# One program for routing and experts, and the last tile's work in another order: a mixture-of-experts layer on one core

## What is computed

```python
x = x + gt1 * (mixed @ w_out)                     # residual, kept in memory as x1
h = rmsnorm(x, g_ffn_norm) * (1 + sc2) + sh2      # kept in memory as h2
logits = h @ w_router + b_router
top_logits, top_idx = lax.top_k(logits, 4); wts = softmax(top_logits)
# for each expert e, for the tokens that chose it:
gu = h[tokens] @ w_gate_up[e] + b_gate_up[e]
act = min(glu, 7) * sigmoid(1.702 * min(glu, 7)) * (clip(lin, -7, 7) + 1)
x[tokens] += gt2 * wts * (act @ w_down[e] + b_down[e])
return rmsnorm(x, g_final)
```

## Time and profile before

| what | value |
|---|---|
| median of 3 runs | 2393.32 us (2392.87 to 2393.83) |
| the profiled execution's own time | 2393.82 us |
| its span, first to last instruction | 2392.2 us |
| PE busy | 2272.3 us (95%) |
| PEld, DVE, ACT, POOL busy | 65%, 40%, 14%, 36% |
| moved by DMA | 526 MB, mean 220 GB/s |

### The profile page before, as it was taken

One profiled execution on the slowest core, in us unless ns is written; L12 is line 12 of the kernel. 1 busy time (PEld: TensorE's weight loads), 2 busy tenths in 40 slices (PEclk: granted clock), 3 DMA queues, 4 the chain that ended last, 5 costly groups with the idle time before them and its releaser, 6 DMA issues. The chain is left out here.

```text
span 2392.2 us, 84238 instructions
## 1 busy us (share of the span) xinstructions
PE 2272.3 (95%) x33744; PEld 1559.7 (65%) x33744; DVE 957.4 (40%) x3183; ACT 335.9 (14%) x917; POOL 857.8 (36%) x1672
## 2 busy tenths in 40 slices
PE   6999999999999699999999999999999999999994
PEld 3878876555544367767777777776776667776563
DVE  2222226776356433333333333333333333333333
ACT  0000006776411100000000000000000000000001
POOL 1100004544214543434343434344443434444333
PEclk8999999999999799999999999999999999999997
DMA  9423042000234687476769494968869988989994
GB/s 314 163 90 109 1 121 71 2 1 2 77 119 145 222 313 278 143 270 210 272 212 340 147 341 145 342 207 297 313 229 384 349 285 303 380 292 390 391 370 160
DMA packets 195573, 526.26 MB, mean 220 GB/s; under 512 B 45416, under 2 KB 75264, under 8 KB 195328
## 3 DMA queue, kind: packets, MB, share of 16 engines
q1 hardware_dynamic: 142496, 479.22, 53.4%
q0 software_dynamic: 33808, 40.21, 8.2%
q10 hardware_dynamic: 19088, 4.47, 0.9%
HBM read 489.98 MB, written 33.35 MB: 219 GB/s over the span
## 5 line engine op out<-in xcount | busy, mean ns | idle before, releaser
L1670 PE MATMUL psum<-w_ring,xT 128*32 128x256 f32 x18304 | 1038.5, 380 | 28.5 <-issue 25.6
L1670 PEld LDWEIGHTS psum<-w_ring,xT 128*32 128x32 f32 x18304 | 693.7, 110 | 322.0 <-issue 48.6
L1682 PE MATMUL psum<-w_ring,actT 128*32 128x256 f32 x9152 | 528.7, 380 | 9.3 <-DMA w_ring<-in_w_down 7.7
L1682 PEld LDWEIGHTS psum<-w_ring,actT 128*32 128x32 f32 x9152 | 329.5, 110 | 166.0 <-DVE actT L1735 36.5
L1599 POOL TENSOR_TENSOR scalars<-scalars 128x1 f32<-128x1 f32 x578 | 109.9, 190 | 749.5 <-DVE xT L1739 657.4
L1717 ACT ACTIVATE sig<-glu 128x128 f32<-128x128 f32 x286 | 88.6, 310 | 1471.4 <-DVE glu L1726 1471.4
L1618 POOL DMA_INDIRECT x_rows<-y_out,scalars_i x145 | 233.9, 1613 | 43.7 <-issue 43.4
L1724 DVE TENSOR_TENSOR psum<-psum,up_bias 128x256 f32<-128x256 f32 x143 | 61.8, 432 | 410.3 <-PE psum L1670 400.1
L1748 DVE SCALAR_TENSOR_TENSOR y_out<-psum,scalars,gate_q 128x256 f32<-128x256 f32 x143 | 69.2, 484 | 300.0 <-PE psum L1682 220.9
L719 POOL TENSOR_SCALAR scores<-scores,coef 128x64 f32<-128x64 f32 (+5 forms) x128 | 133.5, 1058 | 147.7 <-DVE coef L926 147.7
L1608 POOL DMA_INDIRECT x_gathered<-h_rows,scalars_i x144 | 153.5, 1066 | 79.4 <-issue 77.4
(11 more groups left out here) (241 smaller groups left out, 2009.6 us busy)
## 6 DMA issues: line engine op xcount, KB each, us to landing
w_ring<-in_w_gate_up SPq DMA_DIRECT2D x256, 1024.0 KB, 16.0
w_ring<-in_w_down SPq DMA_DIRECT2D x128, 1024.0 KB, 19.9
ada_then_cmp_in<-in_w_ada SPq DMA_DIRECT2D x16, 1024.0 KB, 7.0
ada<-in_w_ada SPq DMA_DIRECT2D x8, 1024.0 KB, 6.9
xt<-in_x SPq DMA_DIRECT2D x8, 512.0 KB, 9.8
w_uv_then_w_out<-in_w_in SPq DMA_DIRECT2D x4, 1024.0 KB, 11.7
x_rows_in<-in_x SPq DMA_DIRECT2D x8, 512.0 KB, 4.2
x_rows<-x SPq DMA_DIRECT2D x8, 512.0 KB, 2.9
```

Of the source, the lines that this page charges most:

```text
L1670: last = nc.tensor.matmul(psU[h][j * BLK:(j + 1) * BLK, :], xT[:, k, :], w[:, j], start=(h == 0 and k == 0), stop=(k == KD - 1))
L1682: last = nc.tensor.matmul(psO[m * BLK:(m + 1) * BLK, :], actT[h][:, k, :], w[:, m * Q:(m + 1) * Q], start=False, stop=(h == 1 and k == KD ...
```

## The change

`experts` is no longer a block of its own. Its five streams become functions (`expert_loads`, `expert_rows`, `expert_products`, `expert_sigmoids`, `expert_gates`) that the streams of `route` call at their end, after a wait until `counts` is written (`s_order` at 3). The `AHEAD` counters and the three additions of nothing are gone, with what cleared and indexed them. DVE makes tile 7's residual before it transposes block 0. TensorE transposes tile 7's rows before the biases and half of block 0's second half. The first weighing waits for no addition.

```diff
@@ sync
+            sp.wait_ge(s_sc[i], 16 * TOPK * TILES // 2)
+        sp.wait_ge(s_order, 3)
+        sp.wait_ge(parts.s_xg, 16 * (FIRST + 1))
+        expert_loads(sp, parts)
@@ gpsimd
-                parts.gather(pool, 0)
-                pool.wait_ge(s_spare, 48)
-                parts.add_nothing(pool)
+                parts.gather(pool, 0, 1)
             if t == KNOWN_TILES + 3:
-                parts.add_rows(pool, 0, 4)
-                parts.gather(pool, 1)
+                parts.gather(pool, 1, 4)
         tiles(pool, body)
         scatter(TILES - 2, 0)
-        parts.add_rows(pool, 1, 10)
         scatter(TILES - 1, 1)
...
         parts.load_rows(pool, 0)
+        pool.wait_ge(s_spare, 48)
+        for i in range(2):
+            pool.wait_ge(s_x1st[i], 16 * TILES // 2)
         parts.take_rows(pool, 0)
         pool.wait_ge(parts.s_ids, 4)
-        parts.gather(pool, 2)
+        parts.gather(pool, 2, 7)
         parts.load_rows(pool, 1)
-        parts.add_rows(pool, 2, 16)
+        parts.add_rows(pool, 0, 10)
+        pool.wait_ge(s_order, 3)
+        expert_rows(pool, parts)
@@ tensor
         parts.up(pe, 0, 0)
+        transpose_h2(TILES - 1, 1)
         pe.wait_ge(s_bias, 6)
         pe.wait_ge(s_chain, base(TILES - 1) + 1)
         parts.up_bias(pe, 0)
         parts.up(pe, 0, 1, 0, KD // 2)
-        transpose_h2(TILES - 1, 1)
...
         parts.bias_and_down(pe, 0, 1)
+        pe.wait_ge(s_order, 3)
+        expert_products(pe, parts)
@@ scalar
+        act.wait_ge(s_order, 3)
+        expert_sigmoids(act, parts)
@@ vector
             residual(t, par)
+            if t == TILES - 1:
+                parts.transpose_x(dve, 0)
...
-            if t == KNOWN_TILES + 2:
-                parts.transpose_x(dve, 0)
...
-        ch.link(nc.vector.tensor_copy(counts[:], blocks_f[:]))
+        nc.vector.tensor_copy(counts[:], blocks_f[:]).then_inc(s_order, 1)
...
         parts.weigh(dve, 1)
-
+        dve.wait_ge(s_order, 3)
+        expert_gates(dve, parts)
@@ weigh
-        dve.wait_ge(s_y, b + AHEAD)
+        if not (isinstance(b, int) and b == 0):
+            dve.wait_ge(s_y, b)
...
-        dve.wait_ge(s_ysc, 16 * b + 16 * AHEAD + 16)
+        if not (isinstance(b, int) and b == 0):
+            dve.wait_ge(s_ysc, 16 * b)
@@ expert_rows (was the gpsimd stream of experts)
-                parts.gather(pool, first + i + 1)
-                parts.add_rows(pool, first + i + 1, 6 * (first + i) + 10)
+            parts.gather(pool, first + i + 1, 6 * (first + i) + 1)
+            parts.add_rows(pool, first + i - 1, 6 * (first + i) + 4)
```

More of the change, by code:

```diff
@@ L35 @@
 FIRST = 2
-AHEAD = 2
 KNOWN_TILES = 4
@@ L150, in layer_kernel @@
             stage3.close()
-            s_w = experts(nc, s4, parts)
         with ExitStack() as s5:
-            combine(nc, s5, sem, s_w, g_final, x1_d, out)
+            combine(nc, s5, sem, parts.s_w, g_final, x1_d, out)
 ADA_CHUNKS = 4
@@ L1494, in expert_parts @@
     HALF = D // 8
-    COLS = MAX_BLOCKS + EDGES + AHEAD + 1
+    COLS = MAX_BLOCKS + EDGES + 1
     xg = sb("x_gathered", [P, Q])
@@ L1507, in expert_parts @@
     ids_x, ids_y, zero_i = (cells_i[:, i:i + 1] for i in range(3))
-    quarter = sb("quarter", [P, 1 + AHEAD])
+    quarter = sb("quarter", [P, 1])
     rows_f = two("slot_rows", [P, EDGES, 2])
@@ L1599, in carry_waits, with gather @@
         nc.gpsimd.tensor_tensor(tick[:], zero[:], zero[:], ALU.add).then_inc(s_steps, 1)
-    def gather(pool, b):
-        done = 6 * b + 1
+    def gather(pool, b, done):
         pool.wait_ge(s_xT, b + 1)
         carry_waits(pool, done)
-        nc.gpsimd.tensor_tensor(ids_x[:], ids[:, bass.ds(b + AHEAD, 1)], zero_i[:], ALU.add).then_inc(s_steps, 1)
+        nc.gpsimd.tensor_tensor(ids_x[:], ids[:, bass.ds(b, 1)], zero_i[:], ALU.add).then_inc(s_steps, 1)
         carry_waits(pool, done + 2)
@@ L1646, in take_rows @@
         pool.wait_ge(s_quarter, e + 2)
-        nc.gpsimd.tensor_copy(ids[:, bass.ds(first + AHEAD, most)], rows_f[e % 2][:, bass.ds(skip, most), 0]).then_inc(s_ids, 1)
+        nc.gpsimd.tensor_copy(ids[:, bass.ds(first, most)], rows_f[e % 2][:, bass.ds(skip, most), 0]).then_inc(s_ids, 1)
         nc.gpsimd.tensor_copy(weight[:, bass.ds(first, most)], rows_f[e % 2][:, bass.ds(skip, most), 1]).then_inc(s_ids, 1)
@@ L1687, in bias_and_down @@
     def bias_and_down(pe, e, n):
-        pe.wait_ge(s_y, n + AHEAD)
+        if not (isinstance(n, int) and n == 0):
+            pe.wait_ge(s_y, n)
         for m in range(4):
@@ L1753, in expert_parts @@
         first_of, many_of, total, weights_of, load_weights, load_rows, load_first_rows, clear)
-    parts.gather, parts.add_rows, parts.add_nothing, parts.take_first_rows, parts.take_rows, parts.load_next, parts.up, parts.bias_and_down = (
-        gather, add_rows, add_nothing, take_first_rows, take_rows, load_next, up, bias_and_down)
+    parts.gather, parts.add_rows, parts.take_first_rows, parts.take_rows, parts.load_next, parts.up, parts.bias_and_down = (
+        gather, add_rows, take_first_rows, take_rows, load_next, up, bias_and_down)
     parts.load_bias, parts.load_gate, parts.sigmoids, parts.gates, parts.transpose_x, parts.weigh, parts.quarter, parts.s_c = (
@@ new lines, in expert_loads, with expert_rows @@
+def expert_loads(sp, parts):
+    for e in range(1, E):
+        w_up, w_dn = parts.weights_of(sp, e)
+        for c in range(CHUNKS):
+            sp.wait_ge(parts.s_w[c], 16 * e)
+            if e >= 2:
+                through = parts.first_of(sp, ENDS[e - 2] + 1)
+                sp.wait_ge(parts.s_spent[c], through)
+            parts.load_weights(sp, e, c, w_up, w_dn)
+def expert_rows(pool, parts):
+    first = parts.first_of(pool, 0)
+    for g in range(N_SEGMENTS):
+        many = parts.many_of(pool, g)
+        after = None
+        if g + 1 < N_SEGMENTS:
+            after = parts.take_rows(pool, g + 1)
+            parts.load_next(pool, g + 1)
+        with pool.Fori(0, many) as i:
+            parts.gather(pool, first + i + 1, 6 * (first + i) + 1)
+            parts.add_rows(pool, first + i - 1, 6 * (first + i) + 4)
+        first = after
+    last = parts.total(pool)
+    parts.add_rows(pool, last - 1, 6 * last + 1)
+    pool.wait_ge(parts.s_ysc, 16 * last)
+    pool.wait_ge(parts.s_xg, 16 * last + 16)
@@ new lines, in expert_products, with expert_sigmoids @@
+def expert_products(pe, parts):
+    for g, (e, part) in enumerate(SEGMENTS):
+        b = parts.first_of(pe, g)
+        many = parts.many_of(pe, g)
+        with pe.Fori(0, many) as i:
+            n = b + i
+            pe.wait_ge(parts.s_xT, n + 2)
+            parts.up(pe, e, 0)
+            parts.up_bias(pe, e)
+            parts.up(pe, e, 1)
+            parts.bias_and_down(pe, e, n)
+def expert_sigmoids(act, parts):
+    parts.load_bias(act, 1)
+    for g in range(N_SEGMENTS):
+        b = parts.first_of(act, g)
+        many = parts.many_of(act, g)
+        with act.Fori(0, many) as i:
+            parts.sigmoids(act, b + i)
+        if g in ENDS and ENDS.index(g) + 2 < E:
+            parts.load_bias(act, ENDS.index(g) + 2)
@@ new lines, in expert_gates @@
+def expert_gates(dve, parts):
+    for g in range(N_SEGMENTS):
+        b = parts.first_of(dve, g)
+        many = parts.many_of(dve, g)
+        dve.wait_ge(parts.s_ids, 2 * g + 4)
+        e = SEGMENTS[g][0]
+        at = HALF_OF[e]
+        dve.wait_ge(parts.s_bias[at], 64 * sum(HALF_OF[p] == at for p in range(e + 1)))
+        with dve.Fori(0, many) as i:
+            n = b + i
+            parts.gates(dve, n, 0, at)
+            parts.gates(dve, n, 1, at)
+            parts.transpose_x(dve, n + 1)
+            parts.weigh(dve, n)
```

88 lines of the change are left out of this document (6 added, 82 removed).

## The result

The changed kernel takes 2383.62 us (median of 7 runs, 2381.15 to 2386.94), the kernel before 2392.87 us beside it (7 runs, 2389.27 to 2393.83): a ratio of 0.9966, with a 95% interval of 0.9955 to 0.9977. It is faster, by 8.1 us of 2392.87 if one goes by the ratio and by 9.3 us if one goes by the medians. A second measurement gave 2380.86 us against 2391.71, a ratio of 0.9947 (0.9933 to 0.9961), which is 12.7 us (by the medians 10.9); the two intervals overlap between 9.3 and 10.8 us. The forecast was 2382.7 us, a gain of 10.6. The profiled execution took 2381.15 us, its span 2379.5.

What follows compares the result with a forecast made beforehand. TensorE was taken to bound the experts' stage, so block 3's start decides: 8.0 us (barrier) + 2.7 (scatters, up to the store) - 0.1 (block 2) = 10.6 us, from 2393.3 to 2382.7 us; range 2378.8 to 2388.2.

Steps and rivals of the forecast that it cites:

- What bounds the kernel: Experts' stage: TensorE, busy 1506.1 of 1529.2 us, sets the pace; the kernel's end moves as block 3's start does.
- The barrier: Between routing and experts: without the drains TensorE starts block 2 when its transposed rows are there; 8.0 us come back.
- The additions of nothing and the order: Ahead of block 2: earlier slots and last scatters on POOL, gain limited by tile 7's store to 2.7 us.
- the store is late next: POOL's wait ahead of the row lists: tile 7's store ends it at 807.5, leaving 2.7 of 7 us won.
- the stores land late: Rival, ahead of block 2: POOL's wait ends at 810.2 as before, only 8 us gained, 2385.3 us; chance 0.08.
- From block 2 to block 3: Block 0's addition lands among expert 1's weights and delays block 2's gates; block 2 takes 13.0 us, price 0.1 us.
- the middle, 5 us: Block 0's addition: assumed landing time after issue, between 2.4 us quiet and 7.7 under load; DVE weighs block 1 at 825.2.
- block 3 at about 831.1: Start of block 3 on TensorE, against 841.73 before: a gain of 10.6 us.
- The held clock: Rival, block 2: higher clock stays and the addition lands in 2.4 us, block 2 takes 10.58 us; 2379.2 us, chance 0.15.
- The held DVE: Rival, block 1's weighing: the first addition holds DVE to 830.7; gain 2.5 to 5.1 us, 2388.2 to 2390.8; chance 0.14.
- The slow loop of landings: Rival, experts' stage: weighing, issue and landing take 10.9 us against TensorE's 10.58; 37 us lost, 2420 us; chance 0.03.
- The weights didn't become the limit: Refers to the no-change rival, experts' stage: weights become the limit, waits for down weights grow by 10 us; chance 0.05.

Runs made afterwards that it cites:

- e6: Changed kernel with the experts as a block of their own again, so with the barrier back, new order kept: 2387.86 us, ratio 0.9980.
- e5: Changed kernel with the last tile's work on DVE and TensorE in its old order, blocks still merged: 2386.04 us, ratio 0.9973.
- e7: Changed kernel with both the barrier and the old order back, so only the additions of nothing are gone: 2385.66 us, ratio 0.9977.
- e1: Changed kernel with SyncE starting expert 1's weights only once block 0's addition has landed: 2381.64 us, ratio 0.9953.
- e10: Changed kernel with expert 1's weights behind block 0's addition and block 3's gather, tile 7's stores ahead of the first expert's last two weight chunks: 2376.80 us, ratio 0.9941.
- e2: Changed kernel with POOL issuing block 0's addition before the next segment's row lists: 2385.54 us, ratio 0.9972.
- e3: Changed kernel with POOL issuing block 0's addition while it waits for the first row lists: 2379.64 us, ratio 0.9950.
- e4: Changed kernel with SyncE starting expert 1's weights earlier, without waiting for block 2's gather: 2387.28 us, ratio 0.9985.

## Why the prediction was right, and where not

The time was right within 1 us, and that is in part luck: the gain forecast at block 3, 10.6 us, was 6.3 there, and 0.9 to 5.6 us were gained behind block 4 for which the prediction has no term and the runs show no cause.

**What bounds the kernel: right.** TensorE's start of block 3 carried through. From block 4 to the last down products no trace differs from another by more than 5.6 us of 1500 (1498.7 to 1504.3), while the marks at block 4 span 14.3 us.

**The barrier: right up to the rows, wrong beyond.** "By this alone 8.0 us come back": with all else in place block 2 moved by 7.3 us (e6 against changed; 7.8 in the second trace), and TensorE started when the rows were there, 0.05 us behind their transposition, not held by its own sequencer. What had stood behind the barrier took 6.2 of these 7.3 back (6.7 of 7.8).

**The additions of nothing and the order: right in sign, held up by another wait than forecast.** Tile 7's slots were to come 2.2 us earlier; they came 1.2 and 1.9 us earlier in the two traces of the changed kernel and 2.8 to 3.2 in the other merged ones of the new order. The last scatter was expected at 800.5, 27.05 us after A, and was issued at 28.4 and 27.6. Its landing was put at 5.5 us, from the earlier trace rows, and the end of POOL's wait at the store, 807.5, which is 34.05 after A. The store landed 31.6 us after A, and POOL went on at 32.3 (32.6 the second time), behind the last scatter. So "the store is late next" is the step that failed here, a small one: block 2 came 43.6 us after A (43.1) where 44.6 was forecast. Nor would an earlier scatter have helped, as e5 shows beside the changed kernel; the prediction let each of the two set the wait by its own issue. The 2.7 us of this term are 4.4 at block 2 in e7 and e6 (3.4 and 1.0), and with the barrier's 7.3 they make the 11.7. The rival that the stores land late, at 36.75 us after A as before, did not come.

**From block 2 to block 3: this step was wrong.** It took a landing of "the middle, 5 us" between 2.4 quiet and 7.7 under load, "since the stream is only starting". It was 8.0 and, in the second trace, 8.8: over the upper end of that range, and as late as in the full stream. With it DVE weighed block 1 at 53.5 us after A, not 51.75, although everything ahead of it was a little earlier. Then "block 3 at about 831.1", 57.7 after A, came at 62.0: the weighing 1.7 us late, 3.2 us and not 2.4 from it to the down products, and from their start to block 3 5.3 us at the lower clock instead of 3.45. The forecast let the clock fall ahead of block 2, after a rest of 2.4 to 5 us; TensorE rested only 0.59 us there (1.49 in the second trace), since block 2's rows came 1.0 and 1.5 us earlier than forecast and, in the first trace, block 1 ended 0.8 us later, and the clock fell in the later wait instead. The gain at block 3 was 6.3 us, not 10.6. The Trainium skill's rule in "DMA: Bandwidth & Descriptors", section "Queues, rings and completion order" (an increment lands only after every earlier write of its DMA engine, across queues) had been weighed there, and the runs agree with it in their direction: 8.0 us with the weights in flight and 2.4 without (e1). The same section of the Trainium skill says that an engine alternates between queues packet by packet, which would also make a small transfer late behind a bulk one; no run here tells the two apart.

**The rivals.** The held clock was right for block 2 (3.66 us) and brought nothing, since the wait behind it was for the addition. The held DVE came true in part: DVE waited 9.91 us for one addition, which cost TensorE 3.20 + 2.28 us, but 4.9 us at most for any later one. The slow loop of landings didn't come: DVE's waits for additions fell from 70.4 to 47.8 us, and from 81.8 to 64.5 in the second traces. The weights didn't become the limit. The stated range begins at 2378.8 us for the held clock, while that rival's own sum gives 2379.2: a slip of 0.4 us that changes nothing.

**Why the time was met nonetheless.** At block 4 the gain is 6.3 us, at the last down products 9.8 in the profiled runs of the first comparison and 7.2 to 11.9 over all pairs of the two traces of each kernel. So 0.9 to 5.6 us came behind block 4, where nothing was forecast. TensorE's waits for down weights are 2.5 to 3.1 us shorter (7.7 and 7.6 before, 5.1 and 4.6 after), which in some pairs is more than the whole of it. How far the weights run ahead of the products doesn't sort these waits: from the first weights of expert 1 to block 4 it is 28.7 us in the changed kernel and only 17.4 in e1, which has 5.8 us of them, fewer than before. Nor do the times follow the marks closely: e1 with block 4 at 65.2 took 2381.64 us, e10 with 66.8 took 2376.80. The rest varies from execution to execution, and why two measurements of one kernel give 8.1 and 12.7 us stays open.

## What to carry to other kernels

A barrier costs its drain, but it also keeps a bulk stream of loads away from the small transfers around it. Whoever removes it should list the small transfers that the next steps wait for and let the bulk stream wait for the last of them: here two waits on SyncE gave 8.0 us at block 4 on top of the change, 4.2 to 6.8 of them left at the last down products. To move the small transfer instead can hand the delay to the next one (e2); put where POOL waited anyway, it cost 1.5 to 2 us on the chain to block 2 and block 3 still came 4.6 us earlier (e3). A landing near the start of a bulk stream is to be costed as one within it.

## What the runs showed of the hardware

An indirect adding transfer of 128 rows of 1 KB landed 2.4 us after its issue ended with no weights in flight, and 8.0 and 8.8 us with weights that had been issued for 1.6 and 1.7 us: the full delay is there from the stream's first megabytes. Issued some 15 us into the stream it landed in 6.0 us (e4). The four transfers of row lists took 1.4 to 2.4 us quiet and 6.3 and 7.3 us under the weights (e4, e2), the gather of block 2 2.1 and 5.8 us (changed, e4).

Ahead of blocks 2 and 3 TensorE kept its higher clock over rests of 0.59, 1.49, 1.52 and 1.87 us (first 64 products 3.66 us). After longer ones there it was slower, but not in the order of their length: 5.30 us after 2.08, 5.35 after 3.59, 5.44 after 8.63, 4.92 after 9.65, 6.30 after 10.25, 5.99 after 11.04, 6.37 after 5.87. In e2 the granted clock was 1.00 before that rest of 2.08 us and 0.50 after it. The rest just before doesn't decide alone. Ahead of block 0, before, one of 2.16 us left the clock at 1.00 (3.66 us, with TensorE busy 4.18 of the 6.5 us before its end), while the one of 1.53 us ahead of block 0's down products came in a stretch in which TensorE was busy 9.11 of 16.5 us at a clock of 0.75, and 6.34 us followed. In the changed kernel two waits of 3.20 and 2.28 us within one block were enough (5.46).
